# A fused transformer kernel whose dense matmuls read and write their 512 token columns in descending order

## The chip, the cores and the metric

The kernel runs on one core of one Trainium2 chip, as one program. The metric is the device time of one execution in microseconds (us), as the median of several runs. TensorE (PE) multiplies matrices out of SBUF into the eight banks of PSUM, VectorE (DVE), ScalarE (ACT) and GpSimd (POOL) do the elementwise work, and SyncE (SP) issues most DMAs. All arithmetic is on float32 data.

## The reference

Two transformer blocks in sequence, on one sequence of 512 tokens with 1024 channels:

```python
# first block, with adaptive scale and shift from c
h = modulate(rmsnorm(x, norm1_g[i]), shift1, scale1)
z = h @ w_in[i] + b_in[i]
y_a = spatial_gating_mixer(gelu(u), gelu(v), ...)       # 8 heads, causal in chunks of 128
y_b = conformer_conv_mixer(val, gate, ...)              # depthwise convolution of width 31
x = x + gate1 * (concatenate([rmsnorm(y_a), rmsnorm(y_b)]) @ w_out[i])
x = x + gate2 * ((silu(g_ff) * up_ff) @ w_ffn_out[i])   # g_ff, up_ff from h2 @ w_ffn_in[i], hidden 2816
# second block: layer 0 is attention (FoX and sparse NSA heads), layer 1 trailing-mean pooling
for layer in range(2):
    m = mixer_fox_nsa(u, ...) if layer == 0 else mixer_pool(u, ...)
    h = h + rmsnorm(m, g[1])
    h = h + rmsnorm(swiglu(rmsnorm(h, g[2]), w_gate, w_up, w_down), g[3])
```

What matters here: nearly all the arithmetic is in dense products of the form (512 tokens x K) by (K x N), with K 1024 or 2816.

## The kernel before

Activations are kept transposed: channels lie in the 128 partitions, the 512 tokens along the free axis, so an activation of 1024 channels is a tile [128, 8, 512] and each `tile[:, k, :]` is one contiguous row of 512 words in each partition. A dense product is cut in blocks of 128 output channels. Each block accumulates in one PSUM bank [128 output channels, 512 tokens], and all 512 columns of the bank are written by every matmul.

A float32 product is made of three products in the type float32r (declared `F32R`). Weight and activation are each split into a high part and a low part, and high x high, high x low and low x high are added in the same bank. The high parts of the weights (`WH`) are written by ScalarE at L305, the low parts (`WL`) by VectorE at L309; both have two buffers and are filled one block ahead while TensorE works on the other. The pairs of activation tiles are `HH`/`HL` (`h_hi`, `h_lo`), `FH`/`FL` (`hid_hi`, `hid_lo`, the hidden layer of the feed-forward parts), `AH`/`AL` (`ao_hi`, `ao_lo`, attention output), `NBH`/`NBL` (`conv_hi`, `conv_lo`) and two `lead` pairs used while a norm is still being computed.

The triples of matmuls stand in five places:

- `block`, L375 to L388, used for most of the kernel: all blocks of the input projection after the second, the feed-forward parts of all three layers, the first attention projections. Blocks alternate between the two banks `PS[0]` and `PS[1]`.
- `part` in `pe_phase_led`, L398 to L402: the first blocks of the first feed-forward part.
- `part` at L1170 to L1174: the first two blocks of the kernel and the output projection of the first block.
- `att_part`, L1366 to L1370: the first block of the attention projections.
- `lin_step`, L1428 to L1441: the attention projections that are interleaved with the attention itself, and the attention's output projection.

Each of these places issues nothing but matmuls and waits on TensorE's queue, in the order of the code. The last matmul of a block raises the semaphore `mm`; on it ScalarE overwrites the weight buffer just used, and ScalarE or VectorE reads the bank, and then raises `ev[0]` or `ev[1]`, for which TensorE waits before it starts the next block in that bank.

Other matmuls on TensorE: float32 ones on unsplit data (L454, L1394), column sums and broadcasts for the norms (L508 to L536), the convolution (L1220), transposes, scores and products of the attention (L1489 to L1545), the pooling (L1601, L1615).

Of the kernel before, what the change touches and what calls it, by code (L numbers as in the profile page):

```python
# [22 lines left out]
C = D // P  # L23
# [50 lines left out]
def build_program(nc, xT, vec, ada_w, w_in, w_out, ffi, ffo, ln_rows, ws, bs, att_w, att_out, bf, pe, w1, w2,  # L74
                  pool_w, f2i, f2o, outT):
    ctx = ExitStack()
    with ctx:
# [14 lines left out]
        HH = sb("h_hi", [P, C, S], F32R)  # L92
# [21 lines left out]
        PS = [ctx.enter_context(nc.psum_tensor(f"bank{i}", [P, S], F32)) for i in range(2)]  # L114
# [260 lines left out]
        def block(n, par, kc, hi, lo, k0, bank, start, stop, ready=None, between=None):  # L375

            pe_ = nc.tensor
            pe_.wait_ge(wlo, n + 1)
            for k in range(kc):
                if ready is not None:  # L380
                    pe_.wait_ge(n_lo, ready + k + 1)
                w_h, w_l = WH[par][:, k * P:(k + 1) * P], WL[par][:, k * P:(k + 1) * P]
                pe_.matmul(bank[:, :], w_h, hi[:, k0 + k, :], start=start and k == 0, stop=False)  # L383
                pe_.matmul(bank[:, :], w_h, lo[:, k0 + k, :], start=False, stop=False)  # L384
                last = pe_.matmul(bank[:, :], w_l, hi[:, k0 + k, :], start=False, stop=stop and k == kc - 1)  # L385
                if between is not None and k < kc - 1:
                    between(k)
            last.then_inc(mm, 1)  # L388

        def pe_phase_led(name, hi, lo, ready, inside_lead, midway):  # L390

            pe_, n, cnt = nc.tensor, N0[name], O0[name] // 2

            def up(g, t):
                nc.tensor.wait_ge(ev[t % 2], cnt + 2 * g + t // 2)
                block(n + 4 * g + t, t % 2, C, hi, lo, 0, PS[t % 2], True, True)

            def part(t, w, h_, l_, k):  # L398
                w_h, w_l = WH[w][:, k * P:(k + 1) * P], WL[w][:, k * P:(k + 1) * P]
                pe_.matmul(PS[t][:, :], w_h, h_[:, k, :], start=k == 0, stop=False)  # L400
                pe_.matmul(PS[t][:, :], w_h, l_[:, k, :], start=False, stop=False)
                return pe_.matmul(PS[t][:, :], w_l, h_[:, k, :], start=False, stop=k == C - 1)  # L402

            def shift_sums(t):
                if t == 0:
                    pe_.wait_ge(lead_sh, 2)
                for k in range(C):
                    for e, w in enumerate((WH[t], WL[t])):
                        m = pe_.matmul(PS[2][:, 2 * t:2 * t + 2], w[:, k * P:(k + 1) * P], SHL[:, k, :],
                                       start=t == 0 and k == 0 and e == 0, stop=t == 1 and k == C - 1 and e == 1,  # L410
                                       skip_group_check=True)
                return m
            for t in range(2):
                pe_.wait_ge(ev[t], cnt)
                pe_.wait_ge(wlo, n + t + 1)
                for k in range(C):
                    if t == 0:
                        pe_.wait_ge(lead_lo, k + 1)
                    part(t, t, LH, LL, k)
                    if t == 0:  # L420
                        inside_lead(k)
                shift_sums(t).then_inc(mm, 1)
            for step in range(C + LAG):
                if step < C:
                    if step == 0:
                        pe_.wait_ge(ev[0], cnt + 1)
                        pe_.wait_ge(wlo, n + 3)
                    pe_.wait_ge(n_lo, ready + step + 1)
                    m = part(0, 0, hi, lo, step)
                    if step == C - 1:  # L430
                        m.then_inc(mm, 1)
                if step >= LAG:
                    if step == LAG:
                        pe_.wait_ge(ev[1], cnt + 1)
                        pe_.wait_ge(wlo, n + 4)
                    m = part(1, 1, hi, lo, step - LAG)
            m.then_inc(mm, 1)
            with nc.tensor.Fori(1, G[name] // 2 + 1) as g:
                for t in range(4):
                    up(g, t)  # L440
            midway()
            with nc.tensor.Fori(G[name] // 2 + 1, G[name]) as g:
                for t in range(4):
                    up(g, t)
# [691 lines left out]
        def _(pe_):  # L1136
# [32 lines left out]

            def part(t, k, hi, lo, first, last):  # L1170
                w_h, w_l = WH[t][:, k * P:(k + 1) * P], WL[t][:, k * P:(k + 1) * P]
                pe_.matmul(PS[t][:, :], w_h, hi, start=first, stop=False)  # L1172
                pe_.matmul(PS[t][:, :], w_h, lo, start=False, stop=False)  # L1173
                return pe_.matmul(PS[t][:, :], w_l, hi, start=False, stop=last)  # L1174

            def first_two():

# [152 lines left out]
            for step in range(CA + 2):  # L1330
                if step < CA:
                    pe_.wait_ge(n_lo, nj["na"].lo + step + 1)
                    m = out_part(0, step)
                    if step == CA - 1:
                        m.then_inc(mm, 1)
                if step >= 2:
                    m = out_part(1, step - 2)
# [27 lines left out]

            def att_part(w, low, k):  # L1366
                w_h, w_l = WH[w][:, k * P:(k + 1) * P], WL[w][:, k * P:(k + 1) * P]
                pe_.matmul(PS[w][:, :], w_h, HH[:, k, :], start=k == 0, stop=False)
                pe_.matmul(PS[w][:, :], w_h, low[:, k, :], start=False, stop=False)
                return pe_.matmul(PS[w][:, :], w_l, HH[:, k, :], start=False, stop=k == C - 1)  # L1370
            n5, cnt5 = N0["att5"], O0["att5"] // 2
            pe_.wait_ge(ev[0], cnt5)
            pe_.wait_ge(wlo, n5 + 1)
# [8 lines left out]
            for k in range(C):  # L1382
                for half, w_ in enumerate((WH[0], WL[0])):
                    m = pe_.matmul(PS[2][:, 0:2], w_[:, k * P:(k + 1) * P], FSH[:, k, :], start=k == 0 and half == 0,
                                   stop=k == C - 1 and half == 1, skip_group_check=True)
# [5 lines left out]
            for k in range(C):  # L1391
                pe_.wait_ge(n_xg, xg5 + k + 1)
                for t in range(2):
                    m = pe_.matmul(PS[3 + t][:, :], RAW[2 + t][:, k * P:(k + 1) * P], XG[:, k, :], start=k == 0,  # L1394
                                   stop=k == C - 1)
# [32 lines left out]
            def lin_step(name, j, k, first=None, last=None):  # L1428
                t, n = j % 2, N0[name] + j
                hi, lo = (AH, AL) if name == "att_out" else (HH, HL)  # L1430
                if first is None:
                    first, last = k == 0, k == C - 1
                if first:
                    pe_.wait_ge(ev[t], O0[name] // 2 + j // 2)
                    pe_.wait_ge(wlo, n + 1)
                w_h, w_l = WH[t][:, k * P:(k + 1) * P], WL[t][:, k * P:(k + 1) * P]
                pe_.matmul(PS[t][:, :], w_h, hi[:, k, :], start=first, stop=False)  # L1437
                pe_.matmul(PS[t][:, :], w_h, lo[:, k, :], start=False, stop=False)  # L1438
                m = pe_.matmul(PS[t][:, :], w_l, hi[:, k, :], start=False, stop=last)  # L1439
                if last:  # L1440
                    m.then_inc(mm, 1)  # L1441

# [1154 lines left out]
```

## Time and profile before

| | |
|---|---|
| median of 3 runs | 1761.01 us |
| lowest and highest | 1759.5 us, 1761.68 us |
| span of the profiled execution, first to last instruction | 1757.1 us |
| median less that span | 3.9 us |
| instructions in the profile | 22185 |
| busy: TensorE matmul, TensorE weight load | 1679.6 us, 1311.8 us |
| busy: VectorE, ScalarE, GpSimd | 916.1 us, 627.2 us, 225.3 us |
| mean granted TensorE clock | 0.983 |

The profile is of one execution; its span is set beside the median of the unprofiled runs. "L383" is line 383 of the kernel. PE is TensorE's matmul, PEld its weight load, which has records of its own. Matmuls are pipelined, so the records of two neighbours overlap, and their ends are modelled: the distance from start to start says more than the duration. The granted clock is a share of 2.4 GHz, with two levels, 1.2 and 2.4 GHz. What stands after "<-" behind an idle time is the instruction that ended it.

### The profile page before, as it was taken

What the parts mean: (1) busy time and instruction counts of PE and PEld (TensorE: products, weight loads), DVE (VectorE), ACT (ScalarE), POOL (GpSimd) and SP (SyncE); (2) the same over time, 40 slices, a digit from 0 to 9 for tenths busy, and PEclk for the clock granted to TensorE, in tenths of its full rate; (3) what the DMA queues carried; (4) which work ended last, traced back from release to release, by engine and by line L of the source; (5) the groups of instructions that cost most, each with busy time, mean ns of one, the idle gap of its engine ahead of it and who ended that gap; (6) DMA issues with size and microseconds to landing.
All of it is one profiled execution on the core that took longest, in us unless ns stands there. A gap on an engine that the chain in (4) does not pass through costs nothing.

```text
span 1757.1 us, 22185 instructions
## 1 busy us (share of the span) xinstructions
PE 1679.6 (96%) x8263; PEld 1311.8 (75%) x8263; DVE 916.1 (52%) x1376; ACT 627.2 (36%) x946; POOL 225.3 (13%) x204
## 2 busy tenths in 40 slices
PE   1999899999999999999999999999998999999996
PEld 1757688888888867666667788888887688888885
DVE  6765676544334463666667544444336644444223
ACT  1324334222223362554555333333226333333221
POOL 5010106998000030000000000003000000000000
PEclk9999999999999999999998999999999899999998
DMA  7565134454332241111101322233211133333221
GB/s 281 204 200 167 40 110 161 169 181 157 109 107 97 69 117 64 37 37 49 37 25 61 108 96 95 95 100 115 98 57 49 61 98 100 99 96 115 92 80 48
DMA packets 48588, 179.27 MB, mean 102 GB/s; under 512 B 5968, under 2 KB 6640, under 8 KB 48272
## 3 DMA queue, kind: packets, MB, share of 16 engines
q1 hardware_dynamic: 43600, 162.04, 27.5%
q0 software_dynamic: 3776, 14.78, 2.7%
q10 hardware_dynamic: 1152, 1.66, 0.4%
q8 instruction: 37, 0.61, 0.1%
q14 instruction: 23, 0.19, 0.0%
HBM read 173.04 MB, written 2.10 MB: 100 GB/s over the span
## 4 chain that ended last, share of the span: by engine, by line
PE 71%; issue 22%; DVE 5%; DMA 1%; ACT 1%; ACTq 1%; POOL 0%; POOLq 0%; DVEq 0%; SPq 0%
PE bank L383 15%; PE bank L385 14%; PE bank L384 14%; PE bank L1437 3%; PE bank L1439 2%; PE bank L1438 2%; PE bank L1545 2%; PE bank L1501 2%; PE bank L1521 2%; DVE ada_acc L1972 1%; PE bank L1172 1%; PE bank L1174 1%; PE bank L1173 1%; PE bank L454 1%; PE bank L1394 1%
## 5 line engine op out<-in xcount | busy, mean ns | idle before, releaser
L309 DVE TENSOR_TENSOR w_lo<-raw,w_hi 128x1024 fp32r<-128x1024 f32 (+1 forms) x229 | 316.4, 1382 | 575.2 <-ACT w_hi L305 574.9
L305 ACT ACTIVATE w_hi<-raw 128x1024 fp32r<-128x1024 f32 (+1 forms) x229 | 258.0, 1127 | 564.4 <-PE bank L385 482.7
L383 PE MATMUL bank<-h_hi,w_hi 128*128 128x512 f32 x1136 | 448.0, 394 | 0.5 <-DVE w_lo L309 0.5
L385 PE MATMUL bank<-h_hi,w_lo 128*128 128x512 f32 x1136 | 442.2, 389 | 0.0
L384 PE MATMUL bank<-h_lo,w_hi 128*128 128x512 f32 x1136 | 442.2, 389 | 0.0
L383 PEld LDWEIGHTS bank<-h_hi,w_hi 128*128 128x128 f32 x1136 | 213.2, 188 | 50.2 <-issue 5.2
L385 PEld LDWEIGHTS bank<-h_hi,w_lo 128*128 128x128 f32 x1136 | 213.2, 188 | 45.0
L384 PEld LDWEIGHTS bank<-h_lo,w_hi 128*128 128x128 f32 x1136 | 213.3, 188 | 44.6 <-issue 1.7
L383 PE MATMUL bank<-hid_hi,w_hi 128*128 128x512 f32 x528 | 205.6, 389 | 0.0
L384 PE MATMUL bank<-hid_lo,w_hi 128*128 128x512 f32 x528 | 205.4, 389 | 0.0
L385 PE MATMUL bank<-hid_hi,w_lo 128*128 128x512 f32 x528 | 205.4, 389 | 0.0
L574 POOL TENSOR_TENSOR stat<-stat,nhalf 128x4 f32<-128x4 f32 x9 | 12.6, 1403 | 1054.3 <-DVE stat L540 1054.3
L383 PEld LDWEIGHTS bank<-hid_hi,w_hi 128*128 128x128 f32 x528 | 99.1, 188 | 20.9 <-issue 0.4
L384 PEld LDWEIGHTS bank<-hid_lo,w_hi 128*128 128x128 f32 x528 | 99.1, 188 | 20.7
L385 PEld LDWEIGHTS bank<-hid_hi,w_lo 128*128 128x128 f32 x528 | 99.1, 188 | 20.5
L1068 POOL TENSOR_SCALAR m_out<-m_out,c_act 128x1024 f32<-128x1024 f32 x24 | 71.1, 2963 | 3.7 <-DMA m_out<-in_ada_w 2.7
L801 ACT ACTIVATE hid_hi<-tmp 128x512 f32 (+1 forms) x44 | 27.9, 633 | 117.2 <-DVE tmp L818 117.2
L1855 ACT ACTIVATE p_t<-bank 128x1024 f32<-128x1024 f32 (+4 forms) x52 | 37.8, 727 | 80.6 <-PE bank L1521 75.2
L1437 PE MATMUL bank<-h_hi,w_hi 128*128 128x512 f32 x128 | 58.8, 460 | 0.0
L798 ACT ACTIVATE tmp<-tmp 128x512 f32<-128x512 f32 x44 | 27.8, 632 | 84.4 <-DVE tmp L811 84.4
L1872 ACT ACTIVATE scores<-scores,att_stat 128x512 f32<-128x512 f32 (+3 forms) x96 | 52.7, 552 | 11.1 <-DVE att_stat L2382 11.1
L820 DVE TENSOR_TENSOR hid_lo<-tmp,hid_hi 128x512 f32 (+1 forms) x44 | 30.5, 693 | 38.6 <-ACT hid_hi L801 38.6
(397 smaller groups left out, 2079.5 us busy)
## 6 DMA issues: line engine op xcount, KB each, us to landing
raw<-in_f2i SPq DMA_DIRECT2D x88, 512.0 KB, 3.3
raw<-in_ffi SPq DMA_DIRECT2D x44, 512.0 KB, 3.4
raw<-in_f2o SPq DMA_DIRECT2D x32, 704.0 KB, 4.0
ada_w<-in_ada_w SPq DMA_DIRECT2D x24, 512.0 KB, 4.3
m_out<-in_ada_w POOLq DMA_DIRECT2D x24, 512.0 KB, 3.7
raw<-in_att_w SPq DMA_DIRECT2D x23, 512.0 KB, 3.3
raw<-in_ffo SPq DMA_DIRECT2D x16, 704.0 KB, 4.0
raw<-in_ada_w SPq DMA_DIRECT2D x16, 512.0 KB, 4.9
```

Source lines behind the costliest of these rows:

```text
L305: nc.scalar.activation(WH[par][:, 0:kc * P], RAW[s][:, 0:kc * P], ACT.Copy).then_inc(whi, count)
L309: nc.vector.tensor_tensor(WL[par][:, 0:kc * P], RAW[s][:, 0:kc * P], WH[par][:, 0:kc * P].bitcast(F32), ALU.subtract).then_inc(wlo, count)
L383: pe_.matmul(bank[:, :], w_h, hi[:, k0 + k, :], start=start and k == 0, stop=False)
L384: pe_.matmul(bank[:, :], w_h, lo[:, k0 + k, :], start=False, stop=False)
L385: last = pe_.matmul(bank[:, :], w_l, hi[:, k0 + k, :], start=False, stop=stop and k == kc - 1)
L1068: pool.tensor_scalar(w, w, CACT[:, i % C:i % C + 1], None, ALU.mult).then_inc(late_mul, 1)
L1437: pe_.matmul(PS[t][:, :], w_h, hi[:, k, :], start=first, stop=False)
L1438: pe_.matmul(PS[t][:, :], w_h, lo[:, k, :], start=False, stop=False)
L1439: m = pe_.matmul(PS[t][:, :], w_l, hi[:, k, :], start=False, stop=last)
L1501: m = pe_.matmul(QB[:, half, 0:L], lhs, rhs, start=kind != "fox", stop=True)
L1855: act.activation(dst[:, :, 0:L], TB[0:rows, :, 0:L], ACT.Copy).then_inc(a6["pt"], 1)
L1872: act.activation(sc, sc, ACT.Exp, scale=-1.0, bias=AST[:, 0, col:col + 1], accum_out=AST[:, 1, col:col + 1]).then_inc(a6["ex"], 1)
```

## The change

In each of the five places both the activation operand and the bank operand get a step of -1 along their 512 columns. The first column that the matmul reads is that of the last token, and the first column that it writes is the last of the bank; the sum that ends in each column is the same as before. The weight operand stays as it is. No other matmul is changed, nor any instruction that reads a bank or writes an activation tile. The whole diff:

```diff
--- before.py
+++ after.py
@@ -380,9 +380,9 @@
                 if ready is not None:
                     pe_.wait_ge(n_lo, ready + k + 1)
                 w_h, w_l = WH[par][:, k * P:(k + 1) * P], WL[par][:, k * P:(k + 1) * P]
-                pe_.matmul(bank[:, :], w_h, hi[:, k0 + k, :], start=start and k == 0, stop=False)
-                pe_.matmul(bank[:, :], w_h, lo[:, k0 + k, :], start=False, stop=False)
-                last = pe_.matmul(bank[:, :], w_l, hi[:, k0 + k, :], start=False, stop=stop and k == kc - 1)
+                pe_.matmul(bank[:, ::-1], w_h, hi[:, k0 + k, ::-1], start=start and k == 0, stop=False)
+                pe_.matmul(bank[:, ::-1], w_h, lo[:, k0 + k, ::-1], start=False, stop=False)
+                last = pe_.matmul(bank[:, ::-1], w_l, hi[:, k0 + k, ::-1], start=False, stop=stop and k == kc - 1)
                 if between is not None and k < kc - 1:
                     between(k)
             last.then_inc(mm, 1)
@@ -397,9 +397,9 @@
 
             def part(t, w, h_, l_, k):
                 w_h, w_l = WH[w][:, k * P:(k + 1) * P], WL[w][:, k * P:(k + 1) * P]
-                pe_.matmul(PS[t][:, :], w_h, h_[:, k, :], start=k == 0, stop=False)
-                pe_.matmul(PS[t][:, :], w_h, l_[:, k, :], start=False, stop=False)
-                return pe_.matmul(PS[t][:, :], w_l, h_[:, k, :], start=False, stop=k == C - 1)
+                pe_.matmul(PS[t][:, ::-1], w_h, h_[:, k, ::-1], start=k == 0, stop=False)
+                pe_.matmul(PS[t][:, ::-1], w_h, l_[:, k, ::-1], start=False, stop=False)
+                return pe_.matmul(PS[t][:, ::-1], w_l, h_[:, k, ::-1], start=False, stop=k == C - 1)
 
             def shift_sums(t):
                 if t == 0:
@@ -1169,9 +1169,9 @@
 
             def part(t, k, hi, lo, first, last):
                 w_h, w_l = WH[t][:, k * P:(k + 1) * P], WL[t][:, k * P:(k + 1) * P]
-                pe_.matmul(PS[t][:, :], w_h, hi, start=first, stop=False)
-                pe_.matmul(PS[t][:, :], w_h, lo, start=False, stop=False)
-                return pe_.matmul(PS[t][:, :], w_l, hi, start=False, stop=last)
+                pe_.matmul(PS[t][:, ::-1], w_h, hi[:, ::-1], start=first, stop=False)
+                pe_.matmul(PS[t][:, ::-1], w_h, lo[:, ::-1], start=False, stop=False)
+                return pe_.matmul(PS[t][:, ::-1], w_l, hi[:, ::-1], start=False, stop=last)
 
             def first_two():
 
@@ -1365,9 +1365,9 @@
 
             def att_part(w, low, k):
                 w_h, w_l = WH[w][:, k * P:(k + 1) * P], WL[w][:, k * P:(k + 1) * P]
-                pe_.matmul(PS[w][:, :], w_h, HH[:, k, :], start=k == 0, stop=False)
-                pe_.matmul(PS[w][:, :], w_h, low[:, k, :], start=False, stop=False)
-                return pe_.matmul(PS[w][:, :], w_l, HH[:, k, :], start=False, stop=k == C - 1)
+                pe_.matmul(PS[w][:, ::-1], w_h, HH[:, k, ::-1], start=k == 0, stop=False)
+                pe_.matmul(PS[w][:, ::-1], w_h, low[:, k, ::-1], start=False, stop=False)
+                return pe_.matmul(PS[w][:, ::-1], w_l, HH[:, k, ::-1], start=False, stop=k == C - 1)
             n5, cnt5 = N0["att5"], O0["att5"] // 2
             pe_.wait_ge(ev[0], cnt5)
             pe_.wait_ge(wlo, n5 + 1)
@@ -1434,9 +1434,9 @@
                     pe_.wait_ge(ev[t], O0[name] // 2 + j // 2)
                     pe_.wait_ge(wlo, n + 1)
                 w_h, w_l = WH[t][:, k * P:(k + 1) * P], WL[t][:, k * P:(k + 1) * P]
-                pe_.matmul(PS[t][:, :], w_h, hi[:, k, :], start=first, stop=False)
-                pe_.matmul(PS[t][:, :], w_h, lo[:, k, :], start=False, stop=False)
-                m = pe_.matmul(PS[t][:, :], w_l, hi[:, k, :], start=False, stop=last)
+                pe_.matmul(PS[t][:, ::-1], w_h, hi[:, k, ::-1], start=first, stop=False)
+                pe_.matmul(PS[t][:, ::-1], w_h, lo[:, k, ::-1], start=False, stop=False)
+                m = pe_.matmul(PS[t][:, ::-1], w_l, hi[:, k, ::-1], start=False, stop=last)
                 if last:
                     m.then_inc(mm, 1)
```

## Rows read from the trace of the kernel before

**Rows 1.** The page, parts 1 and 2: busy us and share, then busy tenths in 40 slices.
```profile
PE 1679.6 (96%) x8263; PEld 1311.8 (75%) x8263; DVE 916.1 (52%) x1376; ACT 627.2 (36%) x946; POOL 225.3 (13%) x204
...
PE   1999899999999999999999999999998999999996
...
PEclk9999999999999999999998999999999899999998
```

**Rows 2.** Groups by form, TensorE: line, names, shapes, count | busy us, mean ns | idle.
```profile
L383 PE MATMUL bank<-h_hi,w_hi 128*128 128x512 f32 x1136 | 448.0, 394 | 0.5 <-DVE w_lo L309 0.5
...
L383 PE MATMUL bank<-hid_hi,w_hi 128*128 128x512 f32 x528 | 205.6, 389 | 0.0
...
L1437 PE MATMUL bank<-h_hi,w_hi 128*128 128x512 f32 x128 | 58.8, 460 | 0.0
...
L1437 PE MATMUL bank<-ao_hi,w_hi 128*128 128x512 f32 x64 | 26.4, 413 | 2.9 <-ACT h_scratch L694 1.5 <-DVE ao_lo L2422 1.4
...
L1172 PE MATMUL bank<-h_hi,w_hi 128*128 128x512 f32 x48 | 20.7, 432 | 5.7 <-DVE h_lo L623 3.7 <-DVE h_lo L621 2.0
...
L1172 PE MATMUL bank<-conv_hi,w_hi 128*128 128x512 f32 x32 | 14.3, 447 | 4.7 <-DVE conv_lo L2065 2.2 <-DVE w_lo L309 1.5 <-DVE x_res L649 1.1
...
L400 PE MATMUL bank<-lead_hi_t,w_hi 128*128 128x512 f32 x16 | 6.9, 433 | 0.0
L400 PE MATMUL bank<-h_hi,w_hi 128*128 128x512 f32 x16 | 6.6, 412 | 0.2 <-DVE h_lo L623 0.2
...
L1368 PE MATMUL bank<-h_hi,w_hi 128*128 128x512 f32 x8 | 3.6, 454 | 0.0
```

**Rows 3.** Timeline of TensorE's matmuls from 1200 us: start us, duration us, instruction.
```profile
1199.71 0.39 PE L384 MATMUL bank<-h_lo,w_hi 128*128 128x512 f32 x1
1199.94 0.39 PE L385 MATMUL bank<-h_hi,w_lo 128*128 128x512 f32 x1
...
1205.84 0.39 PE L384 MATMUL bank<-h_lo,w_hi 128*128 128x512 f32 x1
```

**Rows 4.** Windows in two feed-forward stretches: length, busy us of each engine, clock, DMA.
```profile
1100.00:1200.00 100.00, 100.00 (x443) 82.81 (x442) 46.60 (x57) 31.12 (x37) 0.00 (x0) 1.00 0.31 102
...
1500.00:1600.00 100.00, 100.00 (x443) 82.81 (x442) 46.56 (x56) 31.29 (x37) 0.00 (x0) 1.00 0.30 96
```

**Rows 5.** Waits, who for whom: total us, times, longest us.
```profile
DVE w_lo L309 <- ACT w_hi L305: 574.9, 192, 11.1
ACT w_hi L305 <- PE bank L385: 482.7, 178, 10.6
...
PE bank L489 <- POOL tmp L600: 30.7, 1, 30.7
...
PE bank L518 <- DVE tmp L549: 11.5, 5, 2.5
```

**Rows 6.** Groups by form, window 1100 to 1200 us, TensorE's weight loads.
```profile
L383 PEld LDWEIGHTS bank<-h_hi,w_hi 128*128 128x128 f32 x148 | 27.8, 188 | 5.7
```

**Rows 7.** Below full clock: window 190 to 200, timeline at 196 us, mean clock.
```profile
190.00:200.00 10.00, 6.63 (x29) 5.58 (x30) 4.42 (x7) 1.87 (x3) 1.95 (x2) 0.73 0.01 2
...
196.57 0.63 PE L1173 MATMUL bank<-conv_lo,w_hi 128*128 128x512 f32 x1
...
200.84 0.63 PE L1174 MATMUL bank<-conv_hi,w_lo 128*128 128x512 f32 x1
...
core 0: 1757.1 us, clock 0.983
```

**Rows 8.** Timeline of TensorE's matmuls at 960 us, float32 operands.
```profile
960.27 13.39 PE L454 MATMUL bank<-x_gained,raw 128*128 128x512 f32 x24
```

## Prediction

> **What bounds the kernel now.** I read four views, in this order. First the busy shares and the forty slices: TensorE is busy for 1679.6 us of a span of 1757.1 us, and apart from the first slices nearly every slice stands at nine tenths or more, with the granted clock at nine tenths or more as well [rows 1]. A busy share alone can mislead here, because the recorded end of a matmul is modelled, so I went on to single instructions. In the groups by form the reader should look for the dense matmuls, those whose three factors are the high and low halves of weight and activation. They come as triples, one line each for high by high, high by low, low by high; only the first line of each triple is shown. The counts are 1136 + 528 + 128 + 64 + 48 + 32 + 16 + 16 + 8 = 1976 triples, so 5928 matmuls of 512 columns each [rows 2]. These are exactly the ones that the five hunks of the diff turn round.
>
> Then the timeline of a dense stretch. A group's mean of 389 ns is the life of one matmul, not its price: the next one starts long before. From the start at 1199.71 us to the start at 1205.84 us there are 27 steps, so 6.13 / 27 = 0.227 us from start to start [rows 3]. The price of all dense matmuls at that spacing is 5928 x 0.227 = 1346 us, 77% of the span. In the two hundred-microsecond windows shown, TensorE never stops (100.00 busy), while VectorE is busy for 46.6 us of them and ScalarE for 31.1 and 31.3 us [rows 4].
>
> Last, the waits. ScalarE's high halves of the weights wait 482.7 us in all for the matmuls of L385, and VectorE's low halves follow them; in the other direction TensorE's largest wait is the 30.7 us at the start, and after it 11.5 us in five norms [rows 5]. So nothing hides under anything: each nanosecond added to or taken from a dense matmul goes to the end of the kernel, about 5.9 us for each nanosecond.
>
> **The change part by part.** The edit leaves the number of instructions, semaphores, waits, DMAs and weight loads as they are. No queue is passed and no buffer is freed at another time: a bank is handed to its reader by the last matmul of its group, and that is the same instruction. Every matmul that adds into a bank that is reversed by the diff is itself reversed, so column t of the bank still holds token t. The other matmuls (transposes, the float32 products of L454 and L1394, attention, convolution) stay forward and write banks or groups of their own. Weight loads keep their forward pattern; they take 188 ns each and lie under the matmul before [rows 6]. All that costs nothing, and not because something covers it: it is the same work.
>
> Two accumulating matmuls in sequence meet the same column 512 columns apart, as before: the first column written is then the last of the bank, in both of them. So no new dependence between neighbours arises either, and the distance at which a sum is read back and added to is the one of the row's 0.227 us.
>
> What is left is one unknown: how long 512 columns take when both the activation is read and the bank is written at descending addresses. No row of the trace shows a TensorE operand with a negative step, so I bound it. The time at 2.4 GHz for 512 columns is 213 ns, against 227 ns in the row; 14 ns are spent on something else between matmuls. The lower end is that these go: 5928 x 0.014 = 83 us, and the time would be 1678. I see no reason for it, as the number of columns and of weight swaps stays. The upper end by the nearest rows comes in two steps. In the stretch of 190 to 200 us the mean granted clock is 0.73 of full, thus partly at the lower level, 1.2 GHz; from 196.57 to 200.84 us the dense matmuls start (200.84 - 196.57) / 10 = 0.427 us apart, that is 0.83 ns for each column instead of 0.44 [rows 7]. That is what one matmul costs when columns pass at half the rate. Further off is the float32 form, whose 24 records of 128x512 take 13.39 us, 0.558 us each [rows 8]; it does more arithmetic for each column, so it is an end of the range and not a likely price. I take zero, for this reason: the step from one column to the next is one word of 4 bytes in both directions, the words touched and their neighbourhood in memory are the same set, and every row shows a stream whose rate follows the clock of the array (0.427 against 0.227, almost the 2 to 1 of the levels). A memory side that was the limit at full clock would show it by a rate that doesn't follow the clock. The 14 ns by which it misses the 2 to 1 say how little slack there is to be seen, and that is why the other side stays in the range.
>
> Rules on memory lines bear on this. What the row shows is a rate of 0.44 ns for each column, forward only [rows 3]. The Trainium skill, in Advanced Engine Details and Errata, section Memory Cachelines, says of the bank side that lines are 8 bytes, that any non-contiguous pattern slows matmuls significantly, and that "Every two consecutive elements should be contiguous for best throughput". Read as a rule on order it speaks against this change and is the second rival's cause; read as a rule on lines it doesn't, since columns 511 and 510 share an 8-byte line as 0 and 1 do. The same section gives SBUF lines of 16 bytes that want at least two hits; the reversed read has four hits in each, as before, and by it the sum would stay at zero. No row here decides between the readings.
>
> **Sum.** 5928 x 0 = 0. The profiled execution has a span of 1757.1 us, and the median of the runs is 1761.01 us, so 3.9 us lie around the span. They stay. Forecast 1761.0 us, between 1757 and 1766 if this case holds.
>
> **The rivals.**
> *Half rate (slower).* The read or the write side moves columns in ascending pairs, and a descending pair has to be split, so a column takes two slots. Place: each dense matmul at full clock. Price: 0.427 - 0.227 = 0.200 us each [rows 3, 7]. It decides from the first column on; the only matmuls spared are those at the lower clock, where the array itself is that slow. A mean clock of 0.983 over the span means at most 0.035 x 1757 = 61 us at the lower level [rows 7], some 140 matmuls. So (5928 - 140) x 0.200 = 1158 us, nothing of it covered as TensorE never waits, and the time is 1761 + 1158 = 2919 us. For it: at full clock the columns come closer than anything else in the trace asks for, and there is no backward row to clear it. Against it: pairs are the same pairs of words in both directions.
> *A stall at the turn.* The start of each matmul lies at the far end of the row, and what is exposed between two matmuls now, 14 ns, is exposed twice: 83 us, 1844 us. I let this stand for all prices between nothing and half rate. Against it: successive matmuls jump between rows of different tiles in the forward order too.
> *The float32 rate.* (0.558 - 0.227) x 5928 = 1962 us, 3723 us. Only if two costs add up.
> *The gap goes (faster).* 1678 us, as above. Nothing in the trace speaks for it.
> *The change doesn't do what it says.* If the program builder folds the two reversals away, since the product is the same, the chip sees the old program and the time is 1761. This can't be told from the forecast by the time, and its chance is in the forecast's.
>
> **How the numbers follow.** No change 0.63; half rate 0.24; a price between 0.08; float32 rate 0.03; gap gone 0.02. Within 0.2% (3.5 us, about what a measurement of this kernel can tell from no change) is not all of the first case: I leave 0.02 of it above and 0.01 below. So same 0.60, slower 0.24 + 0.08 + 0.03 + 0.02 = 0.37, faster 0.03. The predicted time is that of the likeliest case, 1761.0 us. Its own range, 1757 to 1766, holds only some 0.63, so the range has to reach to the half rate: 1757 to 2930 us leaves out the float32 rate and the gap gone. It is wide because the cases are two, not because each is vague.
>
> **What would show it.** Right: in the timeline of a dense stretch, steps of 0.227 us from start to start; the group means at 389 ns; the count in a hundred microseconds still 443. Half rate: steps of 0.43 us with a granted clock of 1.00, TensorE still never idle, and the shares of VectorE and ScalarE down by some 40%. A stall at the turn: steps of 0.24 us. If all that is right and the time still moves, look at the matmuls that were not turned, and at the waits of the five norms. The prediction is wrong from the first dense stretch on if it is wrong at all; there is no stage in which only a part of it would fail.

## The result and the profile after

| | before | changed |
|---|---|---|
| median | 1760.26 us (4 runs) | 1794.89 us (4 runs) |
| lowest, highest | 1759.49, 1761.68 us | 1794.16, 1795.35 us |
| ratio, 95% interval | | 1.0194 (1.018 to 1.0209) |
| span of the profiled execution | 1757.1 us | 1793.3 us |

The changed kernel is 1.9% slower, 34.6 us by the medians and 36.2 us by the two spans. TensorE's busy time rose by 36.5 us (1679.6 to 1716.1); no other engine's moved by more than 4.5 us, the weight loads' by 6.2 us. On the page of the changed kernel, the shares of the engines and the slices answer to [rows 1].

```profile
span 1793.3 us, 22185 instructions
PE 1716.1 (96%) x8263; PEld 1318.0 (73%) x8263; DVE 919.4 (51%) x1376; ACT 626.7 (35%) x946; POOL 220.8 (12%) x204
...
PE   1999899999999999999999999999998999999996
...
PEclk9999999999999999999998999999999899999998
```

The groups by form of the changed kernel, TensorE's matmuls (name, shapes, count, busy us, mean ns); [rows 2] has the same of before.

```profile
L383 PE MATMUL bank<-h_hi,w_hi 128*128 128x512 f32 x1136 | 458.3, 403 | 0.5 <-DVE w_lo L309 0.5
L384 PE MATMUL bank<-h_lo,w_hi 128*128 128x512 f32 x1136 | 452.4, 398 | 0.0
...
L383 PE MATMUL bank<-hid_hi,w_hi 128*128 128x512 f32 x528 | 210.2, 398 | 0.0
...
L1437 PE MATMUL bank<-ao_hi,w_hi 128*128 128x512 f32 x64 | 26.9, 420 | 2.9 <-ACT h_scratch L694 1.4 <-DVE ao_lo L2422 1.4
L1438 PE MATMUL bank<-ao_lo,w_hi 128*128 128x512 f32 x64 | 25.5, 398 | 0.0
...
L1220 PE MATMUL bank<-y_shifted,conv_w_tiles 128*32 128x512 f32 x192 | 21.2, 594 | 0.0
```

The forms of L383 to L385, which are 84% of the turned matmuls, are up by 9 ns in the mean of a record, and those of `ao` by 7 to 8. Forms with pauses or with stretches at the lower clock are up by less, L1437 on `h` by 5 (460 to 465) and L1172 on `h` by 1 (432 to 433). The convolution, which was not turned, keeps its 594 ns. The timeline of the same dense stretch as in [rows 3] (start us, duration us):

```profile
1199.64 0.40 PE L384 MATMUL bank<-h_lo,w_hi 128*128 128x512 f32 x1
1199.87 0.40 PE L385 MATMUL bank<-h_hi,w_lo 128*128 128x512 f32 x1
...
1205.94 0.40 PE L384 MATMUL bank<-h_lo,w_hi 128*128 128x512 f32 x1
```

27 steps take 6.30 us, so the matmuls start 0.2333 us apart. [rows 3] gives 6.13 / 27 = 0.2270 us for before; over 300 steps in the middle of a stage the means are 226.67 and 233.33 ns. That is 6.67 ns for each matmul. In windows of the changed kernel (length, TensorE busy and count, clock, DMA share, GB/s):

```profile
1040.00:1140.00 100.00, 100.00 (x430) 1.00 0.29 94
1240.00:1320.00 80.00, 80.00 (x344) 1.00 0.27 93
```

430 matmuls in 100 us with the engine never idle at full clock, where [rows 4] has 443. A count turns into a step as (window + duration) / count: 100.40 / 430 = 0.2335, 100.39 / 443 = 0.2266 us.

In the trace of before, 5252 of the 5928 dense matmuls are followed in less than 229 ns by the next start; the others stand at a change of kind, behind a pause, among the attention's short matmuls or at the lower clock. 5252 x 6.67 ns = 35.0 us, which is the whole difference. At the lower clock nothing is lost, as the timeline of the changed kernel near the start shows:

```profile
54.90 0.63 PE L1173 MATMUL bank<-h_lo,w_hi 128*128 128x512 f32 x1
55.33 0.63 PE L1174 MATMUL bank<-h_hi,w_lo 128*128 128x512 f32 x1
55.76 0.63 PE L1172 MATMUL bank<-h_hi,w_hi 128*128 128x512 f32 x1
56.19 0.63 PE L1173 MATMUL bank<-h_lo,w_hi 128*128 128x512 f32 x1
```

(56.19 - 54.90) / 3 = 0.430 us, and [rows 7] gives 0.427 for the forward read. To the nanosecond, all steps between dense matmuls at this clock are 426 to 428 ns in the trace of before (21 steps) and 425 to 428 ns in that of the changed kernel (23 steps).

So where the loss is was plain at once. Open were: which side costs it, what in the order costs it, and whether it is the direction at all.

### The profile page after: what moved, and what is told of

It reads as the page before. It is cut to its first block, busy times and chain, and to the rows that moved or that the text cites. A ratio compares the mean times of both kernels' runs of the same rounds, so it can differ in the third digit from the quotient of the medians.

```text
span 1793.3 us, 22185 instructions
## 1 busy us (share of the span) xinstructions
PE 1716.1 (96%) x8263; PEld 1318.0 (73%) x8263; DVE 919.4 (51%) x1376; ACT 626.7 (35%) x946; POOL 220.8 (12%) x204
## 4 chain that ended last, share of the span: by engine, by line
PE 72%; issue 22%; DVE 4%; DMA 1%; ACT 1%; POOL 0%; POOLq 0%; DVEq 0%; SPq 0%; ACTq 0%
PE bank L383 15%; PE bank L384 15%; PE bank L385 15%; PE bank L1437 3%; PE bank L1438 2%; PE bank L1439 2%; PE bank L1545 2%; PE bank L1501 2%; PE bank L1521 2%; PE bank L1220 1%; DVE ada_acc L1972 1%; PE bank L1172 1%; PE bank L1173 1%; PE bank L1174 1%; PE bank L454 1%
## 5 line engine op out<-in xcount | busy, mean ns | idle before, releaser
L383 PE MATMUL bank<-h_hi,w_hi 128*128 128x512 f32 x1136 | 458.3, 403 | 0.5 <-DVE w_lo L309 0.5
L384 PE MATMUL bank<-h_lo,w_hi 128*128 128x512 f32 x1136 | 452.4, 398 | 0.0
L385 PE MATMUL bank<-h_hi,w_lo 128*128 128x512 f32 x1136 | 452.2, 398 | 0.0
L383 PEld LDWEIGHTS bank<-h_hi,w_hi 128*128 128x128 f32 x1136 | 214.5, 189 | 56.5 <-issue 5.2
L385 PEld LDWEIGHTS bank<-h_hi,w_lo 128*128 128x128 f32 x1136 | 214.5, 189 | 51.1
L383 PE MATMUL bank<-hid_hi,w_hi 128*128 128x512 f32 x528 | 210.2, 398 | 0.0
L384 PE MATMUL bank<-hid_lo,w_hi 128*128 128x512 f32 x528 | 210.0, 398 | 0.0
L385 PE MATMUL bank<-hid_hi,w_lo 128*128 128x512 f32 x528 | 210.0, 398 | 0.0
L383 PEld LDWEIGHTS bank<-hid_hi,w_hi 128*128 128x128 f32 x528 | 99.5, 189 | 23.9 <-issue 0.4
L385 PEld LDWEIGHTS bank<-hid_hi,w_lo 128*128 128x128 f32 x528 | 99.5, 189 | 23.7
L1437 PE MATMUL bank<-h_hi,w_hi 128*128 128x512 f32 x128 | 59.5, 465 | 0.0
L1438 PE MATMUL bank<-h_lo,w_hi 128*128 128x512 f32 x128 | 51.0, 399 | 0.0
```

Of the source, the lines that this page charges most:

```text
L383: pe_.matmul(bank[:, ::-1], w_h, hi[:, k0 + k, ::-1], start=start and k == 0, stop=False)
L384: pe_.matmul(bank[:, ::-1], w_h, lo[:, k0 + k, ::-1], start=False, stop=False)
L385: last = pe_.matmul(bank[:, ::-1], w_l, hi[:, k0 + k, ::-1], start=False, stop=stop and k == kc - 1)
L1437: pe_.matmul(PS[t][:, ::-1], w_h, hi[:, k, ::-1], start=first, stop=False)
L1438: pe_.matmul(PS[t][:, ::-1], w_h, lo[:, k, ::-1], start=False, stop=False)
```

## Experiments

The steps below are means from start to start over the middle 300 matmuls of a stage, from the traces. The six feed-forward stages (input and output projection of three layers) are long runs of nothing but `block`, so one kernel can try six forms. A kernel with a form for each stage was executed once; its whole time mixes the forms and is not used. In the first stage some other matmuls stand in the middle of the 300, and the two long steps beside them are left out. The ratios of whole kernels are to executions of the kernel before that were made beside them.

### Which side: the read alone, the bank alone

```diff
-pe_.matmul(bank[:, ::-1], w_h, hi[:, k0 + k, ::-1], ...)
+pe_.matmul(bank[:, :], w_h, hi[:, k0 + k, ::-1], ...)      # read alone
+pe_.matmul(bank[:, ::-1], w_h, hi[:, k0 + k, :], ...)      # bank alone
```

> Only the activation is read in descending order; the bank is written in ascending order, so the sums land in the wrong columns and the output is not the reference's. After the change the dense matmuls start 0.2333 us apart, before it 0.2267 us. Theory read: the 6.7 ns belong to the read of the activation, so the time here is that of the changed kernel, 1795 us, steps of 0.2333 us. Theory write: they belong to the write into the bank, so 1760 us and 0.2267 us. If both sides carry a share, something between, 1778 us for equal shares.

> Only the bank is written in descending order, the activation is read in ascending order, so the sums land in the wrong columns. Theory read: 1760 us, steps of 0.2267 us. Theory write: 1795 us, steps of 0.2333 us. If the two sides overlap and each alone costs it, both this and the run with the read alone give 1795 us.

Measured: read alone 1793.13 us, ratio 1.0198 (1.0181 to 1.0215), steps 233.33 ns. Bank alone 1760.76 us, ratio 1.0009 (0.9999 to 1.0018), steps 226.67 ns. Windows of the same stretch, first the read alone, then the bank alone:

```profile
1040.00:1140.00 100.00, 100.00 (x430) 1.00 0.28 91
```
```profile
1040.00:1140.00 100.00, 100.00 (x443) 1.00 0.29 94
```

The whole cost is on the read of the activation: it alone gives the changed kernel's step. Writing the bank from its last column to its first is free.

### Which order: two kernels with a form for each stage

```diff
+if form == "halves":        return ap.rearrange("p (a b) -> p a b", a=2)[:, ::-1, :]
+if form == "lines_down":    return ap.rearrange("p (a b) -> p a b", b=4)[:, ::-1, :]
+if form == "words_down":    return ap.rearrange("p (a b) -> p a b", b=4)[:, :, ::-1]
+if form == "pairs_down":    return ap.rearrange("p (a b) -> p a b", b=2)[:, ::-1, :]
+if form == "in_pairs_down": return ap.rearrange("p (a b) -> p a b", b=2)[:, :, ::-1]
```

> Each feed-forward stage has its own order of columns, the same for read and write, so the sums are right; all else is forward. What counts is the step from start to start in each stage. First input stage: the two halves of 256 columns swapped, ascending inside. Theory start (one cost for each matmul, because its first column lies at the far end): 0.2333 us. Theory direction (cost of descending steps): 0.2267 us. First output stage: 16-byte groups of four columns descend, the columns in a group ascend; direction over groups counts: 0.2333, direction of words counts: 0.2267. Second input stage: groups ascend, the four columns in a group descend; the reverse of that. Second output stage: matmuls by turns descending and ascending; if the cost belongs to each descending matmul, 0.2300 on the mean; if it belongs to the jump back between two descending ones, 0.2267; if a sum that is needed again at once has to be waited for, far above 0.2333. Third input stage: all descending, but as two matmuls of 256 columns each; third output stage: ascending, two of 256 each. Theory fixed cost: 0.1200 us ascending (106.7 + 13.3) and 0.1267 us descending. Theory cost by column: 0.1200 and 0.1233.

> As the run with an order for each stage, with others. First input stage: read descending, write ascending; first output stage: write descending, read ascending (sums in wrong columns in both, so the output is not the reference's): theory read 0.2333 and 0.2267 us, theory write the reverse. Second input stage: ascending in four matmuls of 128 columns; second output stage: descending in four of 128. Fixed cost: 0.0667 (53.3 + 13.3) and 0.0733 us, unless the weight load of each matmul sets a floor above both; cost by column: 0.0667 and 0.0683. Third input stage: pairs of columns descend, ascending within the pair; third output stage: pairs ascend, descending within the pair. If the side that costs works in pairs of columns in an 8-byte word and the order inside a pair counts, 0.2267 and 0.2333; if the order of pairs counts, 0.2333 and 0.2267.

| order of the 512 columns | step, ns |
|---|---|
| halves of 256 swapped, ascending inside | 226.67 |
| groups of 4 descend, words inside ascend | 233.33 |
| groups of 4 ascend, words inside descend | 226.67 |
| by turns descending and ascending matmuls | 230.3 |
| read descends, bank ascends | 233.33 |
| bank descends, read ascends | 226.67 |
| pairs descend, ascending inside | 233.33 |
| pairs ascend, descending inside | 226.67 |
| two matmuls of 256, descending (third input stage, `h` tiles) | 118.33 |
| two matmuls of 256, ascending (third output stage, `hid` tiles) | 120.00 |
| four matmuls of 128, descending; ascending | 111.67; 111.67 |

The windows of the first kernel, groups of 4 that ascend with their words turned, and further down the two widths of 256:

```profile
1040.00:1140.00 100.00, 100.00 (x443) 1.00 0.30 97
...
1450.00:1550.00 100.00, 100.00 (x847) 1.00 0.28 91
1660.00:1740.00 80.00, 80.00 (x669) 1.00 0.23 76
```

Two things follow. The sign of the step is not what costs: it is free inside 16 bytes, and the jump back to the far end of the row is free too (halves). And the cost is neither fixed for each matmul nor in proportion to its columns: at 256 columns the descending read is even 1.67 ns quicker than the ascending one, which neither theory had. Each was measured in one stage and on other tiles, so whether the 1.67 ns belong to the direction or to the place of the tiles isn't shown. At 128 columns both stand at 111.67 ns, far over the 53.3 ns of the columns (128 at 2.4 GHz). That is why the second kernel took 2096.79 us as a whole. With descending and ascending matmuls by turns the mean lies between the two prices, and most single steps are 227, 228, 232 or 233 ns: the price goes with each matmul's own order, and no sum waits for another.

### Blocks of columns

```diff
+ap = ap.rearrange("p (a b) -> p a b", b=b)
+return ap[:, ::-1, :] if kind == "blocks_down" else ap[:, :, ::-1]
```

> Shown so far: the cost of 6.7 ns for each matmul (step 0.2333 us against 0.2267) is on the read of the activation, it comes with groups of 4 columns in descending order and with descending pairs, and it doesn't come with a descent inside a group of 4 nor with two swapped halves. Here blocks of 128, 64, 32, 16 and 8 columns descend in the first five feed-forward stages, ascending inside a block; in the last one blocks of 32 ascend and the 32 columns inside descend. Theory direction (the cost is that of reading down from one 16-byte group to the next): only the last one has steps near 0.2333 us, the blocks of 128 to 32 stay at 0.2267 us and the blocks of 8 lie between. Theory competition (activation and the next weights are read at once, and it is the course of the two addresses over the whole matmul that counts): the cost rises step by step as the blocks get smaller, and 32 descending inside ascending blocks costs little.

Measured: blocks of 128 and of 64 descending 226.67, blocks of 32, 16 and 8 descending 233.33, blocks of 32 ascending with a descent inside 236.67 ns. Windows of this kernel, stages two (blocks of 64), four (16), five (8) and six (descent inside 32):

```profile
520.00:600.00 80.00, 80.00 (x354) 1.00 0.24 81
...
1240.00:1320.00 80.00, 80.00 (x345) 1.00 0.24 78
1450.00:1550.00 100.00, 100.00 (x430) 1.00 0.28 94
1660.00:1740.00 80.00, 80.00 (x340) 1.00 0.21 72
```

340 in 80 us, 80.40 / 340 = 0.2365 us, is the slowest order of all, and it is neither forward nor backward. The direction theory had 226.67 for blocks of 32 and fell. The competition theory fell in its details too: there is no rise step by step, and it had the last order cheap. The border lies between blocks of 32 and of 64 words, 256 bytes: a reordering that leaves the 16-byte groups' places modulo 64 words in sequence is free. That spoke for something that counts places modulo 64 words, and the other reader on TensorE is the weight load, which goes on under the matmuls: in the windows of [rows 4] the weight loads are busy for 82.81 of 100 us in which the matmuls never stop.

### The weight operand

```diff
+if w_order == "step2":   w_h, w_l = (w[:, at:at + 2 * P:2] for w in (WH[par], WL[par]))
+elif w_order == "step0": w_h, w_l = (w[:, at:at + 1].to_broadcast([P, P]) for w in (WH[par], WL[par]))
+else:                    w_h, w_l = (w[:, at:at + w_cols] for w in (WH[par], WL[par]))
```

> The activation is read ascending in the first of each pair of stages and descending in the second, and the weight operand is changed in both (so the sums are not the reference's). First pair: the 128 weight columns are taken at a step of 2 words. Second pair: only 64 weight columns, filling half of the bank's partitions. Third pair: the same weight word 128 times (step 0). Theory direction: descending stays 6.7 ns above ascending in all three pairs. Theory competition: the difference, and the 13.3 ns that an ascending matmul takes over its 213.3 ns of columns, both depend on the weight read: with 64 columns about half of each (0.220 and 0.223 us), with step 0 nothing or nearly nothing (0.2133 in both), with step 2 other values than 0.2267 and 0.2333.

> Fewer weight columns, activation ascending and descending by turns: 1 column, 1 column, 32, 32, 96, 96 (only so many partitions of the bank are filled, the sums are not the reference's). 64 columns gave 0.2300 ascending and 0.2333 descending. Theory competition of the two reads: with 1 column nothing is left to compete, so both directions near 0.2133 to 0.216 us, and 32 columns between. Theory handover (a fixed cost between two matmuls that depends on where the addresses stand when one takes over from the other): with 1 column the two directions still differ by some ns and both stay above 0.2200 us.

| weight words read | ascending activation, ns | descending, ns |
|---|---|---|
| 128 | 226.67 | 233.33 |
| 96 | 230.0 | 233.33 |
| 64 | 230.0 | 233.33 |
| 32 | 231.7 | 233.33 |
| 1 | 231.1 | 233.33 |
| one word 128 times | 231.1 | 233.33 |
| 128 at step 2 | 233.3 | 233.33 |

Neither theory holds as it was put. Less weight traffic makes the ascending read slower, not faster, and never makes the descending one faster. Two stages of the kernel with narrow weights, one weight word; ascending in a timeline with 22 steps in 5.08 us, 0.2309 us each, and descending in a window:

```profile
339.76 0.39 PE L406 MATMUL bank<-h_hi,w_lo 128*1 128x512 f32 x1
...
344.84 0.40 PE L404 MATMUL bank<-h_hi,w_hi 128*1 128x512 f32 x1
```
```profile
520.00:600.00 80.00, 80.00 (x344) 1.00 0.27 88
```

But the direction theory's constant difference is gone as well: 6.7 ns with the weight operand of before, 0 to 3.3 ns with the others of this table.

### Where the weights lie

```diff
+at = k * P + (off if k < kc - 1 else -off)
+w_h, w_l = (w[:, at:at + P] for w in (WH[par], WL[par]))
```

> The activation is read ascending; the weight window is shifted by 4, 8, 16, 32, 64 and 96 words in the six feed-forward stages (so other weights are used, and the sums are not the reference's). Theory direction: 0.2267 us throughout. Theory competition: if what counts is when two reads fall on the same part of the memory, the shift changes it in at least one stage; a step under 0.2267 us would be a way to a faster kernel.

> As the run with the shifted weight window, with the activation read descending (the sums are not the reference's). Theory direction: 0.2333 us throughout. Theory competition: the step changes with the shift in at least one stage.

In the two runs above the last window of a block lies at `-off`, so the values for 4, 8 and 16 words include it; in the two sweeps it is `off - 64`, the same place modulo 64.

> Ascending reads, the weight window shifted by 2, 12, 20, 24, 28 and 40 words in the six feed-forward stages (the sums are not the reference's); the last window of each block is 64 words lower, so that the place modulo 64 words is the same throughout. Theory place: a shift of 2 keeps the same 16-byte groups in meeting and gives 0.2267 us, all the others between 0.230 and 0.2335 us. If the step at shift zero is not the least there is, one of the shifts gives less than 0.2267 us, and with it a way to a faster kernel.

> As the run before, with shifts of 62, 44, 48, 52, 56 and 60 words. Theory place: 0.230 to 0.2335 us, with the values of 60 and 62 nearest to 0.2267 us because they are 4 and 2 words short of a whole period of 64. A step below 0.2267 us in any stage would be a way to a faster kernel.

| shift of the weights, words | ascending read, ns |
|---|---|
| 0, 60, 64 | 226.67 |
| 48 | 228.9 |
| 4 | 226.67 and 233.33, see below |
| 44 | 230.0 |
| 2 | 230.7 |
| 52, 20 | 231.9, 232.0 |
| 32, 96 | 232.4, 232.4 |
| 16 | 233.0 |
| 8, 12, 28, 40, 56, 62 | 233.3 to 233.4 |
| 24 | 234.3 |

With a descending read the shifts of 4 to 96 all give 233.3 to 233.6 ns. Windows of the ascending kernel with shifts of 16 and 64 words:

```profile
1040.00:1140.00 100.00, 100.00 (x431) 1.00 0.28 94
...
1450.00:1550.00 100.00, 100.00 (x443) 1.00 0.29 95
```

The reading is ascending in both; only the weights lie 64 bytes or 256 bytes further on. So an ascending read costs 233 ns or more, as much as the descending one, at eight of the 18 shifts of the table, and loses nothing throughout only at 60 and 64; the kernel before happens to lie at a quickest place. My guess that a shift of 2 words would be free is wrong, and the table isn't smooth. No shift gave less than 226.67 ns, so it offers no faster kernel.

The place isn't all of it. In the stage with a shift of 4 words the same loop with the same operands has two steps, one ahead of eight short matmuls of another kind (L1173) that break in at 386 us, and one behind them:

```profile
300.00:380.00 80.00, 80.00 (x355) 1.00 0.51 172
400.00:480.00 80.00, 80.00 (x345) 1.00 0.37 124
```

80.39 / 355 = 0.2265 and 80.39 / 345 = 0.2330 us; the stage starts near 233 ns, falls to 226.67 after some 70 matmuls with nothing breaking in, holds it for some 410, and holds 233.33 behind the interruption. So the same places can give the quick step or the slow one. The last quick step and the first slow one lie on the two sides of the interruption, but what is carried from matmul to matmul isn't shown. Each value of the table is that of one or two stages. A shift of 32 words shows it on a smaller scale further down. No stage in which all 512 columns are read descending has shown the quick step.

### Is it the relative place?

```diff
+flat = [a[:, :, :].rearrange("p c s -> p (c s)") for a in (hi, lo)]
+at, a_at = k * P + sign * w_off, (k0 + k) * S + sign * a_off
```

> Ascending reads in six feed-forward stages, with the windows of activation and weights shifted by (32, 32), (32, 0), (8, 8), (8, 0), (16, 48) and (64, 0) words in this order (the sums are not the reference's). With the weights alone shifted by 8 and 32 the steps were 0.2333 and 0.2324 us. If only the relative place of the two reads modulo 64 words counts: 0.2267, 0.232, 0.2267, 0.233, 0.232 and 0.2267 us. If the place of the weight window alone counts: 0.232, 0.2267, 0.233, 0.2267, another value, 0.2267. If each operand's place counts by itself: (32, 32) and (8, 8) are above 0.2267 too.

Measured: (32, 32) 226.67; (32, 0) 232.4; (8, 8) 228.1; (8, 0) 233.3; (16, 48) 231.6; (64, 0) 226.67 ns. Both operands shifted alike are as quick as neither. In the stage with (8, 8) the steps inside a block stand at 227 ns and rise only around the block's last window, where the sign of the shift turns and the weights loaded meanwhile are out of place. So what counts, though not alone, is the place of the activation read relative to the weights, modulo 64 words.

### The weight read itself?

> One weight column only, ascending activation; the word lies 63, 16, 32, 48, 60 and 8 words behind the start of its block of 128 in the six stages (the sums are not the reference's). At 0 the step was 0.2314 us. Theory competition for a part of the memory at the moment of the read: a single word can collide for a short time only, so for most of the places the step drops to 0.2267 us or less, and one or two places keep 0.230 or more. Theory handover (the cost doesn't come from the words of the weight read): the same 0.2314 us at all six places.

Measured with a single weight word: 231.7, 231.7, 231.1, 231.1, 231.1, 231.1 ns at 63, 16, 32, 48, 60 and 8 words, and 231.1 at 0 (the 0.2314 us of the expectation had one long step beside another matmul in its mean). A collision of the two reads, word against word, should depend on the place of this word, and the step moves by 0.6 ns only and never drops to 226.67. By its own expectation the handover from one matmul to the next is left, but no view here shows one; see below.

### The whole kernel, both ways round

First the kernel before with every read ascending and the four buffers of split weights moved by 128 bytes:

```diff
+sb("words_before", [P, 32])
 WH = [sb(f"w_hi{i}", [P, KH * P], F32R) for i in range(2)]
 WL = [sb(f"w_lo{i}", [P, KH * P], F32R) for i in range(2)]
+sb("words_behind", [P, 32])
```

> The kernel before, all columns ascending, with one edit: the four buffers of split weights lie 32 words (128 bytes) further on in SBUF, and everything behind them 64 words. With the weight window shifted by 32 words one stage had steps of 0.2324 us against 0.2267. Theory place (what counts is how the places of the two reads, modulo 64 words, meet in time): about 5600 x 5.7 ns = 32 us more, 1792 us, like the changed kernel. Theory direction (only a descending read costs): 1760 us.

Measured 1788.8 us (1786.8 to 1792.08), ratio 1.016 (1.0143 to 1.0177). Its windows in the second layer's input projection and in the third's:

```profile
1040.00:1140.00 100.00, 100.00 (x430) 1.00 0.30 94
...
1450.00:1550.00 100.00, 100.00 (x432) 1.00 0.30 94
```

The steps are 233.33 and 232.39 ns in two stages that issue the same code in the same layout. They are two patterns: 229 and 237 ns by turns in the one, a round of eight steps from 228 to 241 ns in the other. So here too the step isn't settled by the place alone. The runs spread more than those of any other kernel here. This is the control that the case needed: the arithmetic and each access pattern are as before, and 1.6% of the time is lost by where the buffers lie. Everything behind the four moved by 64 words, which by the table is free.

Then the changed kernel with its minus signs kept, but inside groups of four columns, in all five places:

```diff
+def turned(ap):
+    return ap.rearrange("p (a b) -> p a b", b=4)[:, :, ::-1]
-pe_.matmul(bank[:, ::-1], w_h, hi[:, k0 + k, ::-1], ...)
+pe_.matmul(turned(bank[:, :]), w_h, turned(hi[:, k0 + k, :]), ...)
```

> The changed kernel with another order in all five places: groups of 4 columns ascend, the four columns in a group descend, for read and bank alike. In the one stage tried it had steps of 0.2267 us. So 1760 us, equal to the kernel before; about 1795 us if the negative step itself cost something elsewhere in the kernel.

Measured 1760.88 us, ratio 1.0003 (0.9994 to 1.0013). Its timeline has 26 steps in 5.89 us, 0.2265 us each:

```profile
1199.80 0.39 PE L389 MATMUL bank<-h_hi,w_hi 128*128 128x512 f32 x1
1200.03 0.39 PE L390 MATMUL bank<-h_lo,w_hi 128*128 128x512 f32 x1
...
1205.69 0.39 PE L391 MATMUL bank<-h_hi,w_lo 128*128 128x512 f32 x1
```

Negative steps on read and bank cost nothing anywhere in the kernel as long as the 16-byte groups ascend.

## Why the prediction was wrong

- **What bounds the kernel.** Right. The count of 5928, TensorE without a pause and "5.9 us for each nanosecond" carry the result; the last was a tenth too high, as 676 of the matmuls are not followed at the dense step of before. The unchanged instructions and waits were right as well: TensorE's largest waits for other engines are the same to 0.3 us each.
- **The zero.** This is the step that failed: "I take zero". It measured 6.67 ns. The reason given was that the rate follows the clock, so the array is the limit at both levels. But the same paragraph had the number against it: at 1.2 GHz the step is 0.427 us, which is 512 columns and nothing else, and at 2.4 GHz it is 14 ns over its 213 ns. Those 14 ns show only where the columns come fast, and I took them for a fixed cost of changing weights, without a row for that. The runs show that this remainder depends on order and place: 13.3 ns in the layout of before, 20 for the descending read, up to 21 for other places and 23.3 for the worst order. So a rate that nearly follows the clock didn't clear the read. I had kept "how little slack there is to be seen" only for the range.
- **Half rate, 0.24.** Fell. Its cause was a bank or a read that works in ascending pairs; the bank alone costs nothing and pairs turned inside cost nothing. The rule of the Trainium skill that stood beside it (Advanced Engine Details and Errata, section Memory Cachelines) says that any non-contiguous pattern in the bank slows matmuls significantly. These runs disagree for four reordered but dense patterns in the bank: descending alone, ratio 1.0009, and swapped halves, turned groups of four and turned pairs, all at 226.67 ns. None of them leaves gaps in the bank, which no run here tried. Its SBUF half, lines of 16 bytes with at least two hits, is kept by every order tried here and so can't tell 226.67 from 236.67; the border that these runs show is at 256 bytes.
- **A stall at the turn, 0.08, 1844 us with steps of 0.24.** The nearest in size: it too saw the exposed remainder grow. Its mechanism fell, since swapped halves start in the middle and are free, and the size was half of what it said.
- **The float32 rate, 0.03.** Its price was misread. The loop at L454 issues 12 matmuls up to its first break, and the row counts 24 records, so a float32 matmul leaves two records and costs 13.39 / 12 = 1.116 us, not 0.558. Nothing in the forecast hangs on it, as this case lay outside its range already.
- **The range** of 1757 to 2930 us holds 1794.9 us, but only because it had to span two cases; the forecast's own, 1757 to 1766, misses it by 29 us. The chance of slower, 0.37, was nearly all put on prices from +83 us upwards. Between zero and the 14 ns of the row there was room for a small price, and the row that bounds it was in hand.

**What stays open.** Shown: the cost is on the activation read; it depends on the order of places modulo 64 words and, for ascending reads, on the place relative to the weights, though not on this alone; it vanishes at the lower clock. Not shown: why. The single weight word speaks against a collision word by word, and the narrow weights against the volume of the weight read; a descending read holds 233.33 ns under every weight operand and nearly every shift. Why 128 weight words in the right place make an ascending read quicker (226.67) than one word does (231.1 to 231.7) I can't say, nor what makes the same loop keep 226.67 or 233.33 ns at a shift of 4, nor whether direction or place makes two descending matmuls of 256 columns beat two ascending ones.

## What to carry to other kernels

Where TensorE never pauses, the unit to predict is the step from start to start, not the mean duration, and what the step has over its columns is a quantity of its own to be bounded before anything is called free. A few nanoseconds there are 2% of a kernel, and they can be lost without touching an access pattern: a buffer of 128 bytes ahead of the weights did it here. So an edit that moves tiles in SBUF by anything but a multiple of 256 bytes should be checked against the step of a dense stretch, before the difference is put down to the edit's own idea. One such stretch isn't enough, as the same code can hold another step behind an interruption.

## What the runs showed that I had not expected

- With float32r operands, 128 weight columns and all reads ascending, a matmul of 512 columns takes 226.67 ns from start to start, one of 256 takes 120.00, and one of 128 takes 111.67: 13.3 ns over the columns for the first two, 58.3 for the last.
- The place of the weights relative to the activation, modulo 256 bytes, moves the step of 512 columns between 226.67 and 234.3 ns. At a shift of 4 words the same loop held 226.67 ns for some 400 matmuls and 233.33 behind an interruption.
- A descending read takes 233.33 ns with 128, 96, 64, 32 or 1 weight words alike, and 118.33 ns at 256 columns, where the ascending one, in another stage, takes 120.00.
- A PSUM bank can be written in descending order, in swapped halves, or with pairs or groups of four turned inside, at no cost.
